# One-core two-block transformer kernel: mixer results kept in SBUF up to the output product, latent product made per token tile in the stage that sums expert rows, second attention walked in pairs

## The reference, cut to what matters

```python
# first block, token mixer (T = 1024 latent tokens and 256 of context)
s = einsum(q, k) * 64 ** -0.5            # 4 heads, two maps m = 0, 1 of 64 columns each
p = softmax(s)
a = p[:, :, 0] - lam * p[:, :, 1]
a_l = rms_norm(a @ v, da_subln_g) * 0.8  # per head of 128 columns
# gated linear attention: chunks of 64 tokens, forward and backward, 4 heads of 64 / 128
o = mask(q_dec @ k_inv) @ v + q_dec @ state
new_state = state * exp(b_last) + k_to_end.T @ v
g_l = rms_norm(o_forward + o_backward, gla_norm_g) * silu(gr)
y = concat([a_l, g_l]) @ w_out
x = x + gt1 * y                          # gt1, gt2, sh2, sc2: rows of silu(c) @ w_ada + b_ada
h2 = rms_norm(x, norm_ffn_g) * (1 + sc2) + sh2
x = rms_norm(x + gt2 * hier_moe(h2), final_norm_g)   # two expert rows per token
# second block
u = rms_norm(x, norm1_g)
x_r, y_r, c_q, c_kv, k_pe, g_a, g_b = split(u @ w_in)   # c_q, c_kv, k_pe: 576 columns, the latent part
# multi-head latent attention, 8 heads: 128 plain columns and 64 rotary ones in each score
s = (q_nope @ k_nope.T + q_rope @ k_rope.T) * scale     # causal
o = softmax(s) @ v
```

## Time and profile before

| | |
|---|---|
| median of three runs | 3799.47 us (3795.59 to 3799.76) |
| profiled execution | 3797.56 us |
| its span | 3795.8 us |
| PE busy | 3073.5 us, 81% |
| DVE busy | 1769.8 us, 47% |
| ACT busy | 1264.2 us, 33% |
| POOL busy | 281.3 us, 7% |
| mean granted TensorE clock | 0.891 of full speed |

### The profile page before, as it was taken

How to read it: one execution, slowest core, us unless ns; L and a number is a source line. 1 busy time by engine, 2 the same in 40 slices (tenths; PEclk the granted TensorE clock), 3 DMA queues, 4 the chain that set the end, 5 groups by cost and what they waited for, 6 DMA issues and landing times. The chain is left out here.

```text
span 3795.8 us, 40794 instructions
## 1 busy us (share of the span) xinstructions
PE 3073.5 (81%) x14836; PEld 2208.0 (58%) x14836; DVE 1769.8 (47%) x2586; ACT 1264.2 (33%) x1574; POOL 281.3 (7%) x408
## 2 busy tenths in 40 slices
PE   5999878856495999998199789868998895877771
PEld 3888726635474888886177678734666683332330
DVE  4111058846466888886655321245655434111112
ACT  5110025535213777775445310223333320100001
POOL 0000020000001000000100000022000100111111
PEclk7999689968796999999599899989799996999895
DMA  4222287011336999995520131210001446999984
GB/s 183 92 79 74 70 342 304 1 68 36 129 117 230 400 406 405 406 404 224 200 72 17 49 116 64 84 67 7 1 1 42 161 150 264 415 421 420 417 368 183
DMA packets 198949, 710.68 MB, mean 187 GB/s; under 512 B 30728, under 2 KB 66203, under 8 KB 148384
## 3 DMA queue, kind: packets, MB, share of 16 engines
q1 hardware_dynamic: 150720, 589.93, 40.5%
q0 software_dynamic: 23040, 67.14, 4.6%
q10 hardware_dynamic: 25056, 51.82, 3.5%
HBM read 590.94 MB, written 134.64 MB: 191 GB/s over the span
## 5 line engine op out<-in xcount | busy, mean ns | idle before, releaser
L358 DVE TENSOR_TENSOR exp_w_low<-exp_raw,exp_w_high 128x2048 fp32r<-128x2048 f32 x192 | 437.1, 2291 | 70.5 <-ACT exp_w_high L2164 70.5
L2164 ACT CAST exp_w_high<-exp_raw 128x2048 fp32r<-128x2048 f32 x192 | 366.9, 1913 | 135.3 <-PE exp_ps_y L2136 58.4
L2407 PE MATMUL exp_ps_g<-exp_gu,exp_xT 128*64 128x512 f32 x1024 | 265.4, 678 | 89.7 <-DMA exp_gu<-in_exp_w 83.5
L2407 PEld LDWEIGHTS exp_ps_g<-exp_gu,exp_xT 128*64 128x64 f32 x1024 | 88.7, 154 | 246.0 <-issue 210.3
L2110 PE MATMUL exp_ps_g<-exp_w_low,exp_xT_high 128*128 128x512 f32 x512 | 206.7, 404 | 5.7 <-DVE exp_xT_low L358 5.7
L2111 PE MATMUL exp_ps_g<-exp_w_high,exp_xT_low 128*128 128x512 f32 x512 | 203.6, 398 | 0.0
L2112 PE MATMUL exp_ps_g<-exp_w_high,exp_xT_high 128*128 128x512 f32 x512 | 203.6, 398 | 0.0
L366 PE MATMUL inproj_ps<-inproj_w_high,h1T_low 128*128 128x512 f32 (+1 forms) x528 | 202.7, 384 | 0.0
L367 PE MATMUL inproj_ps<-inproj_w_high,h1T_high 128*128 128x512 f32 (+1 forms) x528 | 202.7, 384 | 0.0
L365 PE MATMUL inproj_ps<-inproj_w_low,h1T_high 128*128 128x512 f32 (+1 forms) x528 | 202.6, 384 | 0.0
L2505 DVE TENSOR_TENSOR exp_h<-exp_sg,exp_ps_g 128x256 f32<-128x256 f32 x32 | 19.6, 612 | 341.8 <-ACT exp_sg L2461 341.8
(11 more groups left out here) (555 smaller groups left out, 6870.3 us busy)
## 6 DMA issues: line engine op xcount, KB each, us to landing
exp_gu<-in_exp_w SPq DMA_DIRECT2D x64, 2048.0 KB, 28.4
exp_raw<-in_expert_w_gate SPq DMA_DIRECT2D x64, 1024.0 KB, 6.7
exp_raw<-in_expert_w_up SPq DMA_DIRECT2D x64, 1024.0 KB, 7.2
exp_raw<-in_expert_w_down SPq DMA_DIRECT2D x64, 1024.0 KB, 7.9
exp_dn<-in_exp_w SPq DMA_DIRECT2D x32, 2048.0 KB, 27.2
scratch_y<-da_zero SPq DMA_DIRECT2D x1, 32256.0 KB, 102.2
dap_ada_slab<-in_w_ada SPq DMA_DIRECT2D x16, 1024.0 KB, 7.8
scratch_y<-exp_y ACTq DMA_DIRECT2D x32, 512.0 KB, 8.2
```

Of the source, the lines that this page charges most:

```text
L358: return nc.vector.tensor_tensor(low, x, high.bitcast(F32), ALU.subtract)
L2164: nc.scalar.copy(w_h[:, c], raw[:, b]).then_inc(w_high, 1)
L2407: last = nc.tensor.matmul(ps_g[side(e)], xT[:, m.par, k, side(e)], gu[:, m.buf, :, e, k, :], start=(k == 0), stop=(k == KD - 1))
```

## The change

1. The two mixers' results stay in SBUF as transposed pairs, `mix_da` and `mix_gla`, which `Joined` presents as one; the scratch tensor `mix`, `head_norm` and `turn_rows` go. `turn_normed` scales the first mixer's result tile by tile, turns it and applies the gain, now one value in each partition, while taking the high and low parts. The squares move to ACT, into the attention loop.
2. In the attention loop, the score blocks of map 0 are issued one ahead of those of map 1, and wait for one exponential less.
3. The modulation rows are made in partition 0 alone, stored to the scratch tensor `mod_rows`, and loaded back by four partition broadcasts in the output product's stage (`late`).
4. In the linear attention, gr is loaded in the first Block; the backward advances move into the second, which walks the tiles from the last to the first and also does squares, root, scaling, the product with silu(gr) on POOL, transposes and the two parts.
5. `combine_norms` loads and splits the 576 latent columns of `w_in_2` ahead of its loop, makes their product per tile, copies and stores it; the addition of x moves from DVE to POOL; the expert rows have 3 buffers in place of 4, the x rows 2 in place of 3. The in_c call of `linear` goes.
6. `mla_attention` walks units in pairs with a lag of 4, the rotary scores of two heads issued in turn.
7. `hg` is allocated later and on the right side of SBUF, `keep_early` on the left.

```diff
+                        starts = list(range(0, NK, BANK))
+                        ahead = [(0, n0) for n0 in starts] + [None]
+                        behind = [None] + [(1, n0) for n0 in starts]
                         if u >= 1:
-                            pe.wait_ge(e_done, 2 * u)
-                        for n0 in range(0, NK, BANK):
-                            w = min(BANK, NK - n0)
-                            for m in range(2):
+                            pe.wait_ge(e_done, 2 * u - 1)
+                        for step, pair_of in enumerate(zip(ahead, behind)):
+                            if u >= 1 and step == 1:
+                                pe.wait_ge(e_done, 2 * u)
+                            for m, n0 in filter(None, pair_of):
...
+                    def squares(t):
+                        act.wait_ge(o_read, t + 1)
+                        if t >= 1:
+                            act.wait_ge(squared, t * DA_H)
+                        for h in range(DA_H):
+                            x = t * DA_H + h
+                            nc.scalar.activation(junk[:, h], o[:, t, h], ACT.Square, accum_out=ss[:, 0, x:x + 1]) \
+                                .then_inc(squared, 1)
+
                     for n in range(U + TURN_LAG):
                         turning = 0 <= n - TURN_LAG
+                        if n >= 8 and n % DA_H == 0:
+                            squares(n // DA_H - 2)
...
+def turn_normed(core, name, o, sums, g, mix):
...
+                nc.scalar.activation(sums[:, 1], sums[:, 0], ACT.Sqrt, scale=1.0 / P, bias=core.eps[:]).then_inc(rooted, 1)
+                for i in range(TT):
+                    act.wait_ge(turned, i + 1)
+                    nc.scalar.activation(high[:, :, toks(i)], src(i), ACT.Identity, scale=g[:, 0:1]).then_inc(high_done, 1)
+                act.wait_ge(high_done, TT)
...
+                ch.link(V.reciprocal(sums[:, 2], sums[:, 1]))
+
+                def low_of(i):
+                    dve.wait_ge(high_done, i + 1)
+                    V.scalar_tensor_tensor(low[:, :, toks(i)], src(i), g[:, 0:1], high[:, :, toks(i)].bitcast(F32),
+                                           ALU.mult, ALU.subtract).then_inc(low_done, 1)
+
+                for i in range(TT):
+                    root = sums[:, 2, i * H:(i + 1) * H].unsqueeze(2).broadcast_to([P, H, P])
+                    V.tensor_tensor(o[:, i], o[:, i], root, ALU.mult).then_inc(scaled, 1)
+                    if i >= 2:
+                        low_of(i - 2)
+                low_of(TT - 2)
+                low_of(TT - 1)
...
+                sp.wait_ge(row_taken, 2 * CHUNKS)
+                sp.dma_start(mod_rows, made[0]).then_inc(rows_stored, 16)
+                sp.wait_ge(rows_stored, 16)
...
-                    for m in range(1, 2 * KT):
-                        ch.settle()
-                        advance(1, order_b[m - 1], order_b[m])
...
+        tile_of = lambda n: TT - 1 - n
+        advances = lambda n: 2 * CT + 2 * n
+        OB = 3
...
+                        pe.wait_ge(advanced, 2 * advances(n))
+                        if n >= 2:
+                            pe.wait_ge(scaled, n - 1)
...
+                    for n in range(TT + 3):
+                        if n < TT:
+                            scores(n)
+                        if n >= 3:
+                            turn(n - 3)
+                        if 1 <= n <= TT:
+                            outputs(n - 1)
...
+                    m = 1
+                    for n in range(TT + 4):
+                        if n < TT:
+                            mask(n)
+                            while m <= advances(n):
+                                ch.settle()
+                                advance(order_b[m - 1], order_b[m])
+                                m += 1
+                        if 0 <= n - 2 < TT:
+                            scale(n - 2)
+                        if n >= 4:
+                            take_low(n - 4)
+                    dve.wait_ge(low_done, TT)
...
+                    def root(n):
+                        act.wait_ge(o_done, n + 1)
+                        if n >= 1:
+                            act.wait_ge(squared, n * GLA_H)
+                        for h in range(GLA_H):
+                            nc.scalar.activation(junk[:, h], head(n, h), ACT.Square, accum_out=st[:, n, 0, h:h + 1]).then_inc(squared, 1)
+                        act.wait_ge(squared, (n + 1) * GLA_H)
+                        nc.scalar.activation(st[:, n, 1], st[:, n, 0], ACT.Sqrt, scale=1.0 / GLA_V, bias=core.eps[:]) \
+                            .then_inc(rooted, 1)
+
+                    def take_high(n):
+                        act.wait_ge(turned, n + 1)
+                        nc.scalar.activation(high[:, :, toks(n)], turned_rows(n), ACT.Identity, scale=g[:, 0:1]).then_inc(high_done, 1)
+
+                    for n in range(TT + 3):
+                        if n >= 3:
+                            take_high(n - 3)
+                        if 1 <= n <= TT:
+                            root(n - 1)
...
+                        pool.wait_ge(scaled, n + 1)
+                        rows = o[:, n % OB].rearrange("p h d -> p (h d)")
+                        nc.gpsimd.tensor_tensor(rows, rows, gr[:, tile_of(n)], ALU.mult).then_inc(gated, 1)
...
+                for tile, row in late:
+                    sp.dma_start(tile, row.partition_broadcast(P)).then_inc(late_in, 16)
...
+                if late:
+                    dve.wait_ge(late_in, 16 * len(late))
...
+    YB, XB, IB = 3, 3, 2
...
+                for i in range(YB):
+                    gather(i)
+                for i in range(TT):
+                    pool.wait_ge(added, i + 1)
+                    pool.wait_ge(x_in[i % IB], 16 * (i // IB + 1))
+                    nc.gpsimd.tensor_tensor(r[:, i % 2], r[:, i % 2], xt[:, i % IB], ALU.add).then_inc(x2_ready, 1)
+                    if i + YB < TT:
+                        gather(i + YB)
...
+                for j in range(PARTS):
+                    if j >= 2:
+                        sp.wait_ge(w_split, j - 1)
+                    sp.dma_start(raw[:, j % 2], wv[:, j * EACH:(j + 1) * EACH]).then_inc(w_in[j % 2], 16)
...
+                for j in range(PARTS):
+                    act.wait_ge(w_in[j % 2], 16 * (j // 2 + 1))
+                    nc.scalar.copy(w_h[:, j * EACH:(j + 1) * EACH], raw[:, j % 2]).then_inc(w_high, 1)
+
+                def copy_c(i):
+                    act.wait_ge(c_done, i + 1)
+                    if i >= 2:
+                        act.wait_ge(c_stored[i % 2], 16 * (i // 2))
+                    nc.scalar.copy(c[:, i % 2].rearrange("p (z n) -> p z n", z=2), ps_c[:, i % 2, :, 0:CW]).then_inc(c_copied, 1)
+
+                def store_c(i):
+                    act.wait_ge(c_copied, i + 1)
+                    act.dma_start(c_rows[i * P:(i + 1) * P, :], c[:, i % 2]).then_inc(c_stored[i % 2], 16)
...
+                    if n >= 5:
+                        copy_c(n - 5)
+                        if n >= 6:
+                            store_c(n - 6)
...
-                    ch.link(V.tensor_tensor(rr, rr, gate, ALU.mult))
-                    dve.wait_ge(x_in[i % XB], 16 * (i // XB + 1))
-                    V.tensor_tensor(rr, rr, xt[:, i % XB], ALU.add).then_inc(x2_ready, 1)
+                    V.tensor_tensor(rr, rr, gate, ALU.mult).then_inc(added, 1)
...
+                def product(i):
+                    pe.wait_ge(low_done, i + 1)
+                    if i >= 2:
+                        pe.wait_ge(c_copied, i - 1)
+                    toks = slice(i * P, (i + 1) * P)
+                    for z in range(2):
+                        cols = slice(z * CW, (z + 1) * CW)
+                        last = split_matmuls(nc, ps_c[:, i % 2, z, 0:CW],
+                                             [(high[:, k, toks], low[:, k, toks], w_h[:, k, cols], w_l[:, k, cols])
+                                              for k in range(KD)])
+                    last.then_inc(c_done, 1)
+
+                pe.wait_ge(w_split, PARTS)
+                for n in range(TT + 1):
+                    if n < TT:
+                        turn(n)
+                    if n >= 1:
+                        product(n - 1)
...
-    LAG = 3
+    LAG, HELD = 4, 4
...
+                def plain_scores(n):
                     qt, h = units[n]
-                    keys = (qt + 1) * P
-                    r = slice(64 * (h % 2), 64 * (h % 2) + 64)
-                    q = slice(qt * P, (qt + 1) * P)
                     if n >= 2:
                         pe.wait_ge(e_done, n - 1)
-                    blocks = [slice(k0, min(keys, k0 + BANK)) for k0 in range(0, keys, BANK)]
-                    for k in blocks:
-                        nc.tensor.matmul(ps[:, n % 2, k], qnT[:, h, q], knT[:, h, k], start=True, stop=False)
-                    for k in blocks:
```

(41 more changed lines are left out.)

399 lines of the change are left out of this document (211 added, 188 removed).

## The result

The change made the kernel faster: 3690.7 us (median of 4 runs, 3684.7 to 3694.3) against 3797.5, a ratio of 0.9718 (95% interval 0.9701 to 0.9735). The forecast was 3713, with a range of 3676 to 3760. The profiled execution took 3684.7 us with a span of 3683.0, 112.8 less than the span before; the forecast of its parts was 84.6 less.

What follows compares the result with a forecast made beforehand. Stages stand one behind the other, so each was read by itself, not by TensorE's 81% busy time. Terms 2.2 - 6 - 6.5 - 51 + 36 - 62.3 + 3 = -84.6 took 3797.6 to 3713 us, range 3676 to 3760.

Steps and rivals of the forecast that it cites:

- Rows through memory: End of preparing stage: storing the gate rows and waiting costs 2.2 us (0 to 4); their late loads cost 0.
- Attention loop: First attention: the new score order shortens a unit from 7.22 to about 7.0 us, -6 over 31 units (-19 to +9).
- Linear attention: Last forward state to output product: 54.5 us against 105.6, backward advances hidden under PE, -51 (-58 to -42).
- Sum of expert rows: Summing stage with the latent product inside: head +8, period +13.5, end +14.5, together +36 us (+20 to +55).
- The lock between VectorE and POOL: Summing stage: if POOL's add waited for a whole VectorE pass per tile, 10 us more; by the row's half microsecond, 4.
- Latent stage: The separate latent product stage disappears with its loads, casts, products and stores: -62.3 us, neighbouring stages unmoved.
- Second attention: Walk in pairs: 9.80 us a pair against 9.94 at six key tiles, +3 us in all (-31 to +25).
- one and two about nothing: Second attention: query tiles with one or two key tiles neither gain nor lose from the paired walk.
- Packing pays: Rival, 14%: second attention gains fully from rotary scores running two by two, -31 in place of +3, 3680 us.
- The half clock in the summing stage: Rival, 9%: the latent product runs at half clock in the stage that sums expert rows, +50, 3763 us.
- the chain bind the linear attention: Rival, 9%: the second block's new chain takes 8 us a tile in place of 5.1, +23, 3736 us.
- the second attention lose its clock: Rival, 4%: PE's new waits drop the second attention's granted clock to 1.2 GHz, +105, about 3818 us.

Runs made afterwards that it cites:

- e1: The changed kernel with the first attention's score matmuls in their old order, both maps of a block together: 3705.4 us, ratio 0.9761.
- e3: The changed kernel with the addition of x in the stage that sums expert rows back on VectorE: 3683.6 us, ratio 0.9704.
- e2: The changed kernel with the second attention's walk of the kernel before (single units, lag 3): 3694.9 us, ratio 0.9734.
- e5: The changed kernel with the second attention's rotary scores issued one head after the other: 3690.4 us, ratio 0.9717.
- e6: The changed kernel with ACT's order in the second attention made exponential, copy, exponential, copy: 3672.1 us, ratio 0.9664.
- e9: As e6, but each head's rotary scores stand behind its own plain scores, apart from the other head's: 3694.1 us, ratio 0.9725.
- e11: The changed kernel with the edits of e3 and e6 together: 3664.0 us, ratio 0.9643.
- e7: The changed kernel with the linear attention's backward states advanced at the end of the first Block again: 3701.4 us, ratio 0.9752.
- e8: The changed kernel with x and gains loaded ahead of the latent weights and the weights' splits inside the summing loop: 3689.5 us, ratio 0.9717.
- e4: The changed kernel with the latent product in its own stage again and the old stage that sums expert rows: 3718.9 us, ratio 0.9804.
- e10: The changed kernel with the edits of e3, e6 and e8 together: 3660.4 us, ratio 0.9639.

## Why the prediction was right, and where it was off

The forecast was 22 us above the median and 28 above the profiled execution, to which the parts belong. Of the 28, some 13 are full clock that came earlier or lasted longer than before at two places (5 in the attention loop, 8 in the second attention), which no term had; 9 are the order of the scores, worth 15 and not 6; 6 are stages that the change does not touch; the other terms make up the small rest. Which time the loop gets differs between profiled executions with the same loop code, so that its 5 are luck.

*Rows through memory*: right, +3.4 in the profile and not 2.2, of which 1.8 because the last row itself came later there (538.09 in place of 536.27 for its second half); its store was issued at 538.85 and the next stage started 2.1 us later. The late loads were on time by less than was thought: they landed 29.7 us after the output stage's first issue, where the first sum started at 29.2 before; it started at 29.9. So a term put at 0 was up to 0.7. That stage took 1.0 more.

*Attention loop*: a step that failed. "The chain of PE comes to about 7.0 us against 7.22" was too long by 0.2, and the first and last units were left out. The 0.8 added for a lone first and a lone last block is 0.4 in the rows (2.79 against 2.42). In the steady walk 28 units gained 0.42 each, 12 us in place of 6, and e1 shows that this is the order. The first three gained 5.4: 3.3 by the order, at 1.2 GHz (27.5 to 24.2 in e3), and 2.1 because the clock rose before the third one (22.1). The last 3.2 are the tail from the last unit's maximum on, 18.7 us in place of 21.8; it is 21.8 to 21.9 in e2, e3, e5, e6, e9 and e11, where the clock had fallen before the last results. So the order gave 15 us, within the bounds, and the clock 5. The -20.3 that came is past the range's end of -19; the whole stayed in range because this was one term of seven.

*Norm*: right in size and by its parts (16.7 against 17).

*Linear attention*: right, 53.5 us for 54.5, with a tile at 4.86 for 5.1; e7 shows that the 38 advances are covered, 9.95 us if they are not.

*Sum of expert rows*: right in its sum (+37.7 for +36) by two errors that cancel. Head: 20.8 for 21.5, as worked out. Period: +1.13 for +1.25, ACT's copy and store cost 0.6 and not 1.2 from the sixth step on, and eight tiles have seven periods between them and not eight, so 9.2 in all and not 13.5. End: "two products, a copy and a store's landing" were 14.5; it was 21.3, since four products are left. The low part of a tile comes three steps behind its sum, so that the product of tile 0 starts at 1784.7 and the last sum is at 1812.5, with only three products made. e3 shows that the period through POOL's add is in the chain: the add on VectorE is worth 8.8 us.

The lock between VectorE and POOL was weighed the wrong way round. The row was read as a small delay, and the sum with a whole VectorE pass of waiting for POOL was 10 higher. In the rows after, POOL's add is not delayed (2.34), and VectorE's pass beside it takes 3.39 for 1.28: it is VectorE that stands still for about as long as POOL runs. The Trainium skill (Trainium Architecture — The Big Picture, What this means for kernel authors) has an exclusive lock there, and these rows and e8's agree with it. The earlier trace rows does too, read with its times: VectorE's pass started at 2946.38, POOL's add ended at 2947.01, so that only 0.63 us were left of it, and the pass lost 0.5. The delay was small because the overlap was. The lock costs the stage little: the add on VectorE takes 1.1 us less than POOL's, and e3's period is shorter by about as much (7.77 against 8.91).

*Latent stage*: -60.1 with the recurrent branch, which was 2.2 us longer in this profile (231.3 to 233.4) and 0.3 to 1.6 in the others; the latent stage itself was 62.3. e4 shows 22.3 us for the part as a whole, against 26 forecast.

*Second attention*: the working by query tile held (+0.9, +0.6, +0.2, -0.2, -0.5, -1.1 a pair from three to eight key tiles, against +1.1, +0.7, +0.3, -0.14, -0.5, -1.0), and its two stretches with it: 4.65 and 5.01 at six key tiles for 4.83 and 4.97. The step that failed is "one and two about nothing": one key tile is 2.5 us longer, which no run here takes apart, and at two the full clock comes after 20 us of the stage in place of 44, worth 8.0. Without two key tiles the stage is 2.3 longer, for +3 forecast. e2 and e9 show that the earlier rise goes with the rotary scores standing side by side. The three walks in which they stand apart (before, e2, e9) have the clock at 0.50 for 41.0 us; the ten in which they adjoin have it so for 17.1 (seven profiles), 20.5 (e6) and 27.3 us (e10, e11). The late ones are those in which PE shows no gap. Why the less busy ones get the clock earlier is not settled here, nor why e10 and e11, with e6's walk, get it later than e6.

*The rivals.* "Packing pays" was right in its cause and wrong in its place: packing is worth 18 us at equal clock (e9 against e6), and the changed kernel's order on ACT gives most of it away, as the sum had it. The half clock in the summing stage did not come: 1.00 from 1786 on, though PE stood idle for 1.2 to 1.7 us behind three of the products. In e2, with the same stage, it was back at 0.50 for 3.4 us (from 1827.1), and that stage took 125.2 us in place of 123.9. Nor did the chain bind the linear attention, or the second attention lose its clock; there it gained.

## What to carry to other kernels

When one engine's order is changed, follow the other engines' hand-written orders too: here the pairs gained at four and five key tiles only once ACT's copies stood between its exponentials (17 us for the whole stage). When work is hidden beside a loop, ask when its first operand is ready, not only whether it fits the period: what starts three steps late is still to be done when the loop ends, here four of eight products. And an add that is moved to an idle engine still costs its longer duration wherever the loop's chain runs through it. Where the granted clock changes inside a stage, compare the stage in several executions before its gain is put down to an edit: 5 of the loop's 20 us were not the edit's.
